# Where 32 of the 48 modulation row tiles are loaded and multiplied: beside the first projections, or in the merge and mixer stages

## The reference, cut to what matters

```python
mod = jax.nn.silu(c) @ w_ada[layer] + b_ada[layer]
mod_c = jax.nn.silu(c_ctx) @ w_ada[layer] + b_ada[layer]
sh1, sc1, gt1, sh2, sc2, gt2 = jnp.split(mod[:, None, :], 6, axis=-1)
h = modulate(rms_norm(x_lat, norm1_g[layer]), sh1, sc1)
hc = modulate(rms_norm(x_ctx, norm1_g[layer]), sh1c, sc1c)
mix, mix_c = token_mixer(h, hc, ...)       # attention, gated linear attention, merge, w_out
x_lat = x_lat + gt1 * mix
h = modulate(rms_norm(x_lat, norm2_g[layer]), sh2, sc2)
x_lat = x_lat + gt2 * conv_ffn(h, ...)
```

## Time and profile before

| | us |
|---|---|
| median of 3 runs | 3172.78 (3172.05 to 3173.76) |
| span of the profiled execution | 3172.5 |
| TensorE busy | 3061.5 (97%) |
| VectorE busy | 1439.1 (45%) |
| ScalarE busy | 685.2 (22%) |
| GpSimd busy | 2066.4 (65%) |

### The profile page before, as it was taken

How to read it: one execution, slowest core, us unless ns; L and a number is a source line. 1 busy time by engine, 2 the same in 40 slices (tenths; PEclk the granted TensorE clock), 3 DMA queues, 4 the chain that set the end, 5 groups by cost and what they waited for, 6 DMA issues and landing times.

```text
span 3172.5 us, 38462 instructions
## 1 busy us (share of the span) xinstructions
PE 3061.5 (97%) x13536; PEld 2473.9 (78%) x13536; DVE 1439.1 (45%) x1875; ACT 685.2 (22%) x1191; POOL 2066.4 (65%) x2056
## 2 busy tenths in 40 slices
PE   5889999989999999999999999999999999999998
PEld 3767547868888788888878888888888887888886
DVE  7877752267554673322225322255422236542222
ACT  3244551111002442111122211000211114421110
POOL 4623206756667677777667777778777776777774
PEclk8989999999999999999999999999999999999999
DMA  6711103223222223232222222222232222322221
GB/s 254 252 35 34 34 7 113 96 77 100 95 98 99 94 94 99 93 99 96 99 97 87 100 94 98 96 97 98 95 98 95 99 93 93 106 93 99 93 99 67
DMA packets 86025, 306.71 MB, mean 97 GB/s; under 512 B 9552, under 2 KB 10064, under 8 KB 85648
## 3 DMA queue, kind: packets, MB, share of 16 engines
q1 hardware_dynamic: 82512, 297.73, 27.8%
q10 hardware_dynamic: 3392, 7.28, 0.7%
HBM read 302.87 MB, written 2.10 MB: 96 GB/s over the span
## 4 chain that ended last, share of the span: by engine, by line
PE 90%; DVE 7%; ACT 2%; issue 1%; SPq 1%; DMA 1%; ACTq 0%; DVEq 0%
PE acc L1557 84%; PE side L731 1%; DVE rec_rec_x L1980 1%; PE acc L709 1%; DVE ada_more L1131 1%; SPq L515 1%; DMA xc<-in_ctx 1%; PE acc L616 0%; PE side L1557 0%; PE side L719 0%; DVE prob L1335 0%; PE acc L631 0%; DVE att_stat L1326 0%; PE stat L1620 0%; DVE n_scaled L1108 0%
## 5 line engine op out<-in xcount | busy, mean ns | idle before, releaser
L1519 POOL TENSOR_TENSOR w_lo<-w_raw,w_hi 128x512 fp32r<-128x512 f32 x513 | 672.0, 1310 | 1038.0 <-PE acc L1557 1009.6
L1557 PE MATMUL acc<-h_hi,w_hi 128*128 128x512 f32 x2224 | 877.0, 394 | 30.8 <-ACT gq L846 11.6
L1557 PE MATMUL acc<-h_lo,w_hi 128*128 128x512 f32 x2224 | 869.7, 391 | 0.0
L1557 PE MATMUL acc<-h_hi,w_lo 128*128 128x512 f32 x2224 | 869.2, 391 | 0.0
L1520 POOL TENSOR_TENSOR w_lo<-w_raw,w_hi 128x512 fp32r<-128x512 f32 x513 | 709.0, 1382 | 0.0
L1557 PEld LDWEIGHTS acc<-h_hi,w_hi 128*128 128x128 f32 x2224 | 419.7, 189 | 131.5 <-issue 15.7
L1557 PEld LDWEIGHTS acc<-h_lo,w_hi 128*128 128x128 f32 x2224 | 420.1, 189 | 85.1 <-issue 1.9
L1557 PEld LDWEIGHTS acc<-h_hi,w_lo 128*128 128x128 f32 x2224 | 419.7, 189 | 85.3
L1508 POOL TENSOR_SCALAR w_hi<-w_raw 128x512 fp32r<-128x512 f32 x513 | 404.2, 788 | 37.3 <-DMA w_raw<-in_weights 37.3
L1949 DVE TENSOR_TENSOR x<-acc,x 128x512 f32 (+1 forms) x160 | 110.7, 692 | 661.5 <-PE acc L1557 661.4
L1557 PE MATMUL acc<-mlp_hid_hi,w_hi 128*128 128x512 f32 x1024 | 398.3, 389 | 0.0
(11 more groups left out here) (345 smaller groups left out, 3560.1 us busy)
## 6 DMA issues: line engine op xcount, KB each, us to landing
w_raw<-in_weights SPq DMA_DIRECT2D x513, 512.0 KB, 3.3
ada<-in_ada SPq DMA_DIRECT2D x36, 512.0 KB, 5.4
ada_more<-in_ada SPq DMA_DIRECT2D x10, 512.0 KB, 18.2
x<-in_x ACTq DMA_DIRECT2D x16, 256.0 KB, 6.7
out<-x SPq DMA_DIRECT2D x8, 256.0 KB, 2.2
cvec<-in_cvec ACTq DMA_DIRECT2D x1, 1024.0 KB, 6.1
ada_n<-in_ada SPq DMA_DIRECT2D x2, 512.0 KB, 17.4
xc<-in_ctx SPq DMA_DIRECT2D x1, 1024.0 KB, 16.7
```

The lines of the kernel that those rows point to most:

```text
L1519: pool.tensor_tensor(w_lo[:, slot, 0:half], w_raw[:, slot, 0:half], w_hi[:, slot, 0:half].bitcast(F32), ALU.subtract)
L1557: ins = pe.matmul(out, lhs, rhs, start=start, stop=stop, skip_group_check=group)
```

## The change

Tiles 0 to 15 stay where they are. Tiles 16 to 47 go to a new buffer `late` of four slots, which lies in memory that the attention has used; ScalarE's queue loads them, and a fresh copy of c (`late_vec`) with its own Silu. The 32 products stand at the end of merge steps 1 to 7 (three each) and of mixer steps 0 to 5 (two each, one in the last). The sum with the bias and `gain2` are made in two parts: gt1 after the merge loop, the rest in mixer step 5. The loads of x move behind the first two Sigmoids. SyncE's queue holds panels only, each four ahead of GpSimd.

```diff
-LEAD = 16
+LATE_ADA = 6 * KT - ADA_FIRST
+MERGE_ADA, MIX_ADA = 3, 2
...
+                    late = ft("late", [P, ADA_SLOTS, D])
+                    late_vec = ft("late_vec", [P, D])
...
+        def late_through_merge(m):
+            return min(MERGE_ADA * m, LATE_ADA)
+        def late_through_mix(k):
+            return min(late_through_merge(KT - 1) + MIX_ADA * k, LATE_ADA)
         def first_block_sp(sp, load_panel):
             for m in range(ADA_FIRST):
-                load_ada(m)
+                sp.dma_start(ada_slot[m], io["ada"][m]).then_inc(ada_in[m], 16)
             sp.dma_start(xc[:, :, :], io["ctx"]).then_inc(ctx_in, 16)
             for n in range(SLOTS):
                 load_panel(sp, n, n)
-            for n in range(SLOTS, 2 * SLOTS):
-                sp.wait_ge(panel_made, n - SLOTS + 1)
-                load_panel(sp, n % SLOTS, n)
-            for i, m in enumerate(range(ADA_FIRST, 6 * KT)):
-                load_ada(m)
-                if i % 4 == 3:
-                    n = 2 * SLOTS + i // 4
-                    sp.wait_ge(panel_made, n - SLOTS + 1)
-                    load_panel(sp, n % SLOTS, n)
...
@@ ScalarE, after the last attention head @@
-            for k in range(KT):
-                act.dma_start(x[:, k, :], io["x"][:, k, :]).then_inc(x_in, 16)
+            def load_late(first, last):
+                for i in range(first, last):
+                    if i >= ADA_SLOTS:
+                        act.wait_ge(late_used, i - ADA_SLOTS + 1)
+                    act.dma_start(late[:, i % ADA_SLOTS, :], io["ada"][ADA_FIRST + i]).then_inc(late_in[i % ADA_SLOTS], 16)
+            act.wait_ge(att_turned, UNITS)
+            act.dma_start(late_vec[:, :], io["cvec"][:, 0, :]).then_inc(late_vec_in, 16)
+            load_late(0, ADA_SLOTS)
             act.activation(rec_cl[:, 0, :], table[...], ACT.Exp, scale=-1.0).then_inc(rec_cl_exp, 1)
             act.wait_ge(rec_cl_exp, 1)
             act.activation(rec_cl[:, 1, :], rec_cl[:, 0, :], ACT.Ln, bias=col("one")).then_inc(rec_cl_ln, 1)
+            act.wait_ge(late_vec_in, 16)
+            act.activation(late_vec[:, :], late_vec[:, :], ACT.Silu).then_inc(late_silu, 1)
             for m in range(KT):
...
                 take(o, gate_m[:, m % 2, :], func=ACT.Sigmoid)
                 take(o + 1, gate_g[:, m % 2, :], func=ACT.Sigmoid)
+                if m == 0:
+                    for k in range(KT):
+                        act.dma_start(x[:, k, :], io["x"][:, k, :]).then_inc(x_in, 16)
+                if m >= 2:
+                    load_late(ADA_SLOTS + late_through_merge(m - 2), ADA_SLOTS + late_through_merge(m - 1))
                 act.wait_ge(mg_made, m + 1)
...
             for k in range(KT):
+                done = late_through_merge(KT - 2) if k == 0 else late_through_mix(k - 1)
+                load_late(min(ADA_SLOTS + done, LATE_ADA), min(ADA_SLOTS + late_through_mix(k), LATE_ADA))
                 wait_taken(act, OUT_MIX + k)
                 sq(k, 2, x)
...
@@ VectorE @@
+            def late_products(first, last):
+                for i in range(first, last):
+                    if i == 0:
+                        dve.wait_ge(late_silu, 1)
+                    dve.wait_ge(late_in[i % ADA_SLOTS], 16 * (i // ADA_SLOTS + 1))
+                    w = late[:, i % ADA_SLOTS, :]
+                    dve.scalar_tensor_tensor(out=w, in0=w, scalar=1.0, in1=late_vec[:, :], op0=ALU.mult, op1=ALU.mult,
+                                             accum_out=products[:, ADA_FIRST + i, 0:1]).then_inc(late_used, 1)
+            def late_mod(first, last):
+                dve.wait_ge(late_used, last)
+                a, b = ADA_FIRST + first, ADA_FIRST + last
+                link(dve.tensor_tensor(mod[:, a:b, 0], products[:, a:b, 0], table[:, names["b_ada"] + a:names["b_ada"] + b], ALU.add))
@@ VectorE, after hc is made, and after glow @@
-            for m in range(ADA_FIRST, ADA_FIRST + KT):
-                ada_product(m, 0)
...
-            for m in range(ADA_FIRST + KT, 6 * KT):
-                ada_product(m, 0)
-            link(dve.tensor_tensor(mod[:, ADA_FIRST:, 0], products[:, ADA_FIRST:, 0],
-                                   table[:, names["b_ada"] + ADA_FIRST:names["b_ada"] + 6 * KT], ALU.add))
-            own(dve.scalar_tensor_tensor(out=gain2[:, 0:KT], in0=mod[:, 4 * KT:5 * KT, 0], ...), gains_made, 3)
@@ VectorE, end of each merge step m, and after the loop @@
+                if m:
+                    late_products(late_through_merge(m - 1), late_through_merge(m))
+            late_mod(0, KT)
@@ VectorE, end of each mixer step k @@
+                late_products(late_through_mix(k), late_through_mix(k + 1))
+                if late_through_mix(k) < LATE_ADA <= late_through_mix(k + 1):
+                    late_mod(KT, LATE_ADA)
+                    own(dve.scalar_tensor_tensor(out=gain2[:, 0:KT], in0=mod[:, 4 * KT:5 * KT, 0], ...), gains_made, 4)
@@ SyncE, the panel loop @@
-            lead = SLOTS if start_x else LEAD
+            lead = SLOTS
```

More of the change, by code:

```diff
@@ L430, in build @@
         ada_used = sem("ada_used")
+        late_in = [sem(f"late_in{s}") for s in range(ADA_SLOTS)]
+        late_used = sem("late_used")
+        late_vec_in = sem("late_vec_in")
+        late_silu = sem("late_silu")
         ctx_in = sem("ctx_in")
@@ L504, in build @@
         queries = [qe[:, :], ada[:, ADA_SLOTS - 1, D - T:D]]
-        def ada_free(m):
-            return ADA_FIRST + 2 + m - ADA_FIRST + 1 if m < ADA_FIRST + ADA_SLOTS else 2 * ADA_FIRST + m - ADA_FIRST - ADA_SLOTS + 1
+        def late_through_merge(m):
+            return min(MERGE_ADA * m, LATE_ADA)
+        def late_through_mix(k):
+            return min(late_through_merge(KT - 1) + MIX_ADA * k, LATE_ADA)
         def first_block_sp(sp, load_panel):
[L511 to L515, removed]
             for m in range(ADA_FIRST):
-                load_ada(m)
+                sp.dma_start(ada_slot[m], io["ada"][m]).then_inc(ada_in[m], 16)
             sp.dma_start(xc[:, :, :], io["ctx"]).then_inc(ctx_in, 16)
@@ L1062, in first_block_act @@
                 if k == 0:
-                    act.wait_ge(gains_made, 4)
+                    act.wait_ge(gains_made, 3)
                     wait_made(act, o - 1)
@@ L1117, in ada_product @@
             def ada_product(m, s):
-                slot = m if m < ADA_FIRST else m % ADA_SLOTS
+                out = ada_slot[m]
                 if s == 0:
-                    dve.wait_ge(ada_in[slot], 16 if m < ADA_FIRST else 16 * ((m - ADA_FIRST) // ADA_SLOTS + 2))
-                out = ada_slot[slot]
-                if s == 0 and m < ADA_FIRST:
+                    dve.wait_ge(ada_in[m], 16)
                     out = (spare, spare_b)[m % 2][:, :]
@@ L1130, in ada_product @@
                 made[0] += 1
-                dve.scalar_tensor_tensor(out=out, in0=ada_slot[slot], scalar=1.0, in1=cvec[:, s, :], op0=ALU.mult,
+                dve.scalar_tensor_tensor(out=out, in0=ada_slot[m], scalar=1.0, in1=cvec[:, s, :], op0=ALU.mult,
                                          op1=ALU.mult, accum_out=products[:, m, s:s + 1]).then_inc(ada_used, 1)
+            def late_products(first, last):
[10 more added lines that the diff above has]
+                link(dve.tensor_tensor(mod[:, a:b, 0], products[:, a:b, 0], table[:, names["b_ada"] + a:names["b_ada"] + b], ALU.add))
             def gains(s):
@@ L1171, in first_block_dve @@
                 out_taken[(OUT_MISC + 1) % BANKS], 1)
-            for m in range(ADA_FIRST + KT, 6 * KT):
-                ada_product(m, 0)
-            dve.wait_ge(ada_used, made[0])
-            link(dve.tensor_tensor(mod[:, ADA_FIRST:, 0], products[:, ADA_FIRST:, 0],
-                                   table[:, names["b_ada"] + ADA_FIRST:names["b_ada"] + 6 * KT], ALU.add))
-            own(dve.scalar_tensor_tensor(out=gain2[:, 0:KT], in0=mod[:, 4 * KT:5 * KT, 0], scalar=1.0,
-                                         in1=table[:, names["norm2"]:names["norm2"] + KT], op0=ALU.add, op1=ALU.mult),
-                gains_made, 3)
             own(dve.tensor_tensor(gain2[:, KT:2 * KT], table[:, names["final1"]:names["final1"] + KT],
-                                  table[:, names["norm_mix"]:names["norm_mix"] + KT], ALU.mult), gains_made, 4)
+                                  table[:, names["norm_mix"]:names["norm_mix"] + KT], ALU.mult), gains_made, 3)
             dve.wait_ge(side_made, 1)
@@ L1379, in first_block_dve @@
                     add_up(k - 1, 2)
+                late_products(late_through_mix(k), late_through_mix(k + 1))
+                if late_through_mix(k) < LATE_ADA <= late_through_mix(k + 1):
+                    late_mod(KT, LATE_ADA)
+                    own(dve.scalar_tensor_tensor(out=gain2[:, 0:KT], in0=mod[:, 4 * KT:5 * KT, 0], scalar=1.0,
+                                                 in1=table[:, names["norm2"]:names["norm2"] + KT], op0=ALU.add, op1=ALU.mult),
+                        gains_made, 4)
```

## The result

The changed kernel takes 3179.19 us (median of 20 runs, 3178.05 to 3180.94) against 3173.23 for the kernel before (20 runs, 3171.71 to 3178.07): ratio 1.0018, 95% interval 1.0011 to 1.0024, or 3.5 to 7.6 us more. That is slower by more than the measurement is uncertain, though just under the 0.2% (6.3 us) that I had called the bound, and 0.7 us above my range. The profiled execution has a span of 3177.6 us, against 3172.5. Of 97 executions of the kernel before, over all sessions, 22 lie at 3177.8 to 3179.2 us and the others at 3171.4 to 3175.8; no trace shows one of the long ones, so their cause stays open.

What follows compares the result with a forecast made beforehand. TensorE was taken to bound the moved work's front stretch and the merge and mixer stages. 3172.5 + 0 (front) + 0.95 (entry) + 0 (merge) + 0 (mixer) = 3173.45, so 3173.7 us against the runs' median; range 3171 to 3178.5.

Steps and rivals of the forecast that it cites:

- the bound: Whole kernel: the measurement tells 0.2%, about 6.3 us, from no change; chance of staying within it 0.89.
- Front, 0: Before the merge stage: removing 32 VectorE products gains 0 us, since they lay beside TensorE; bounds -1.1 and +0.5.
- Entry, +0.95: Merge stage entry: five issues, two table loads and a Silu start the first Sigmoid 0.95 us later; bounds -0.3, +3.4.
- Merge steps, 0: Merge steps 1 to 7: three products, 5.4 us, hide in VectorE's 9.74 us of idle time; cost 0.
- Mixer steps, 0: Mixer stage: VectorE's backlog ends at 651.0, just ahead of 651.19; cost 0, bounds 0 to +6.9 us.
- the rival: Mixer stage, 611 to 651 us: VectorE comes out late, deciding from 1.8 us a product; 0 to 6.9 us, chance 0.22.
- GpSimd: Mixer steps: GpSimd needs 5.54 us a panel against 5.43, lagging 0.1 us a step, with some 8 allowed.
- The base: Whole kernel: the forecast against the profiled span, 3173.45, raised to 3173.7 because the span lies 0.28 under the runs' median.

Runs made afterwards that it cites:

- front_only: The changed kernel with the 32 moved products and everything that feeds them left out; 3172.76 us, ratio 0.9994 to the kernel before.
- back_only: The changed kernel with the 32 products run twice, in front as before and again at the new place; 3180.56 us, ratio 1.0016 to the kernel before.
- before_psum: The kernel before, with a PSUM copy of silu(c_ctx) for the 16 front products that use it; 3164.82 us against 3173.42, ratio 0.9968.
- merge_four: The changed kernel with four products in each merge step, leaving four for the mixer stage; 3176.07 us, ratio 1.0007 to the kernel before.
- psum_vec: The changed kernel with Silu behind step 0's Sigmoids, four products a merge step, and merge products reading Silu(c) from PSUM; 3172.54 us, ratio 0.9998.
- after: The changed kernel as first measured and traced; 3179.19 us against 3173.23 for the kernel before, ratio 1.0018.
- after_again: The changed kernel, unedited, run again for a second trace; 3180.16 us against 3174.64 for the kernel before, ratio 1.0016.

## Why the prediction was wrong

The sum had 0.95 us at the entry and 0 elsewhere. The traces show 2.8 to 2.9 at the entry and 2.6 to 3.0 in the mixer stage.

**Front, 0: right as far as can be seen.** `front_only` and `back_only` agree with it, and `zb` still follows ScalarE's logarithm; a gain of about 1 us would be hidden in the spread of the traces.

**Entry, +0.95: right in mechanism, short in size.** Two table loads and a Silu of 1.06 stand where I had put them, and the first Sigmoid comes 1.25 us later behind `om_hi`, not 0.95. The missing 0.3 is the issues: from `om_hi` to Exp it is 2.65 us, forecast 2.33. TensorE's wait grew by as much. That c came in time was in part luck: it took 4.5 us, not my 3.3, and landed as the table load ended. What the sum lacked is the 1.6 us of half clock behind it, which didn't follow the wait of 0.6 here (before, `front_only`, `before_psum`) and followed the one of 1.8 to 1.9 in all four traces that had it. That the two go together at this place is shown; when a wait brings half clock in general is not (one of 1.56 was followed by it in one trace, one of 1.55 in another was not), nor was the wait varied alone. The drain of about 1.38 us that the Trainium skill (ScalarE: Activation LUTs, What ACT_TABLE_LOAD costs) adds to each load is not in the trace: the load starts 0.02 after the Ln ends, load and Silu start 1.29 apart, load and Sigmoid 1.30. Leaving it out was right.

**Merge steps, 0: right.** Three products of 1.52, 1.63 and 2.30 are hidden; `merge_four` hides a fourth.

**Mixer steps, 0: this step failed.** I priced a product at 1.79 us and came out at 651.0 against 651.19. The start was right: the first `gated_add` begins at 620.11 - 0.94 = 619.2 by the clock of before (0.94 is the shift from the entry), as forecast. From its end to the last `gated_add` I allowed 31.0; it took 654.57 - 620.88 = 33.7:

- eleven products, from start to next start, 23.65 instead of 19.7: +3.95
- six pairs of `gated_add` and `add_up` 1.39 instead of 1.5 each: -0.7
- bias sum and `gain2` 1.73 instead of 2.3: -0.6

That makes VectorE 2.4 late. TensorE's wait for `square_sum` grows by 2.1, and the two matmuls behind it take 1.65 instead of 1.12 us: 2.6 in this trace. In the three others they take about 2.0, and the loss is 2.9 to 3.0.

The 1.79 was a mean over mixed company: 14 products in a row, of which the first two began before GpSimd set in at 60.97. VectorE in order of time, before:

```profile
59.46 1.22 DVE L1131 SCALAR_TENSOR_TENSOR ada<-ada,cvec 128x1024 f32<-128x1024 f32 x1
...
61.75 2.31 DVE L1131 SCALAR_TENSOR_TENSOR ada<-ada,cvec 128x1024 f32<-128x1024 f32 x1
...
63.99 2.30 DVE L1131 SCALAR_TENSOR_TENSOR ada<-ada,cvec 128x1024 f32<-128x1024 f32 x1
...
66.22 1.62 DVE L1131 SCALAR_TENSOR_TENSOR ada_more<-ada_more,cvec 128x1024 f32<-128x1024 f32 x1
...
67.77 1.62 DVE L1131 SCALAR_TENSOR_TENSOR ada_more<-ada_more,cvec 128x1024 f32<-128x1024 f32 x1
```

The twelve with GpSimd beside them take 84.53 - 61.75 = 22.78 us, 1.90 each. That alone is above the 1.8 from which I had the rival decide: 14 x 0.11 = 1.5 more on my sum. In a mixer step each product starts while a part of a panel is being made, since both engines repeat with one period, and so meets the contention every time: 2.14 and 2.23. The rival that I had named, with 0.22, had the right place and decided from 1.8 us; I should have priced it from the upper half of the products in company, as I had VectorE busy for 5.1 and GpSimd for 5.54 of each 5.43 us, so that they could not keep out of each other's way. `merge_four` shows that the products in these steps are the cause: with four instead of eleven behind the first `gated_add` the loss is gone. That GpSimd is what makes them long is shown in the merge steps (`psum_vec`) and carried over to the mixer steps.

Behind the earlier trace rows I had found that the port that VectorE and GpSimd share costs less than a full lock, with 4.2 products in 7.56 us; the rows above show four (two of 2.23 and two of 1.55, from start to start). Here a step holds 3.72 us of GpSimd's work alone and two products of 1.22 (1.14 from start to start), 6.0 to 6.15 in a row, and takes 5.75: it overlaps by 0.25 to 0.4. The Trainium skill (SBUF — State Buffer, SBUF: two separate sides) says that the shared ports are locked by a VectorE operation with two inputs in SBUF, against a GpSimd operation that reads SBUF. `psum_vec` agrees with that condition. A lock held for the whole instruction, as the page has it, comes near, but the 0.25 to 0.4 us a step are left over. Taken at its word for the mixer stage, that rule (6.0 to 6.15 a step against TensorE's 5.43) would have given the right sign.

**GpSimd**: 5.75 a step, not 5.54; not a wait of its own on TensorE's path.

**The base.** I added 0.28 us to the span. In eleven profiled executions the time is 1.9 to 2.2 above the span (3179.53 for 3177.6 here), so the profiled execution of before took an estimated 3172.5 + 2.0 = 3174.5, 1.7 above the median of its runs. The forecast didn't suffer from it: span and 0.28 together are the median of the runs, 3172.78, and the longer series has 3173.23.

## What to carry to other kernels

Where a stage has less than 0.1 us a step to spare, price an operation by its company there, not by a mean from elsewhere: two engines that repeat with one period meet at the same point each time. If a two-input VectorE operation on SBUF runs beside GpSimd, look for a free PSUM bank for one operand, first where someone waits: here it gave 8.6 us, where moving 32 products gave none that could be measured. When a wait of TensorE grows, look at the granted clock in the slices behind it.

## What the runs showed that I had not expected

- TensorE fell to half clock within about 1 us behind a wait of 1.8 to 1.9 us and had its full clock back some 3.4 us later, at a cost of 1.6 us, in four traces of four; behind the wait of 0.6 at the same place it did not. Elsewhere a wait of 1.56 was followed by a lower clock in one trace, and one of 1.55 in another was not.
- Reading one operand from PSUM made a 128x1024 product of fp32 1.216 us in all 28 cases, against 1.52 to 2.30 from SBUF beside GpSimd, and GpSimd's two `w_hi` halves of a panel 0.78 and 0.62 instead of 1.09 and 0.98.
- Two traces of one kernel (`after`, `after_again`) differ by 1.9 us before `om_hi` and by 1.6 us behind `root`, so an effect of 1 us shows in distances between landmarks, not in a span.
